# Four gate chunks computed inside the attention stage, and a weight product spread over its output chunks

## The reference

```python
for i in range(DEPTH):                       # DEPTH = 2
    shift, scale, gate = adaln_params(c, ada_w[i], ada_b[i])   # silu(c) @ w + b
    h = rms_norm(x, norm_g[i]) * (1.0 + scale) + shift
    # i = 0: q, k, v, g = split(h @ w_in); q, k normed and rotated;
    #        o = softmax over the last 128 keys, with a sink per head; branch = (o * silu(g)) @ w_out
    # i = 1: v, g = split(h @ w_in); pooled = trailing means of v over 2, 4, 8, 16 tokens, less v;
    #        mixed = einsum(pooled, w_group) * scale;  branch = (mixed * silu(g)) @ w_out
    x = x + gate * branch
```

## Time and profile before

| what | value |
|---|---|
| median of three runs | 1508.71 us (1503.67 to 1509.82) |
| the profiled execution's own time | 1503.65 us |
| its span, first to last instruction | 1501.9 us, mean granted clock 0.993 |
| TensorE busy | 1428.2 us, 95% of the span |
| gate stage's last matmul to slot 20 | 557.1 to 653.8 us of the span |

### The profile page before, as it was taken

The page is one execution under the profiler, slowest core; times in us unless marked ns, Lnnn a source line. Parts: engine busy times, 40 slices in busy tenths (PEclk is TensorE's granted clock), DMA queues, the critical chain, the costliest instruction groups (busy, mean ns, idle before and its releaser), DMA issues.

```text
span 1501.9 us, 20206 instructions
## 1 busy us (share of the span) xinstructions
PE 1428.2 (95%) x7240; PEld 1207.5 (80%) x7240; DVE 881.7 (59%) x1524; ACT 529.3 (35%) x1270; POOL 406.4 (27%) x551
## 2 busy tenths in 40 slices
PE   2899999999999998899999999899999999999999
PEld 1678888788778887888988988788888888888887
DVE  7777666765443449876776774525555443555522
ACT  2443443333311128765555562322213122221200
POOL 2333333321222216555655563310000100000000
PEclk9999999999999999999999999999999999999999
DMA  8655555434998788657767757731121552112142
GB/s 317 217 186 193 192 188 198 180 134 167 341 339 328 276 325 315 239 205 287 287 229 289 276 191 264 240 98 43 42 77 53 182 183 73 43 42 77 51 153 84
DMA packets 96787, 285.62 MB, mean 190 GB/s; under 512 B 10768, under 2 KB 40496, under 8 KB 87088
## 3 DMA queue, kind: packets, MB, share of 16 engines
q1 hardware_dynamic: 87760, 250.74, 46.2%
q0 software_dynamic: 8928, 33.59, 6.4%
HBM read 196.22 MB, written 88.08 MB: 189 GB/s over the span
## 4 chain that ended last, share of the span: by engine, by line
PE 71%; DMA 9%; DVE 8%; issue 5%; POOL 3%; ACT 3%; SPq 1%; POOLq 0%; DVEq 0%; ACTq 0%
PE po_f_ps L1841 23%; PE po_y_ps L1857 12%; PE at_y_ps L1413 9%; PE ga_g_ps L929 8%; PE qk_proj L663 7%; PE at_o_ps L1397 5%; PE at_s_ps L1369 3%; DMA values_split<-qk_late 3%; DMA ga_ada<-in_ada_w 2%; DMA po_xn<-x_mid_t 2%; POOL at_pt L1143 2%; PE at_tr L1379 1%; DMA ga_raw<-in_attn_w_gate 1%; POOL qk_rq L306 1%; DVE qk_late L476 1%
## 5 line engine op out<-in xcount | busy, mean ns | idle before, releaser
L1841 PE MATMUL po_f_ps<-po_ht,po_w 128*128 128x512 f32 x1536 | 348.9, 389 | 0.0
L1841 PEld LDWEIGHTS po_f_ps<-po_ht,po_w 128*128 128x128 f32 x1536 | 288.1, 188 | 60.1 <-DVE po_ht L1703 0.3
L663 PE MATMUL qk_proj<-qk_w_qkv,qk_ht 128*128 128x512 f32 x1152 | 280.4, 399 | 6.8 <-DVE qk_w_qkv L539 4.0
L663 PEld LDWEIGHTS qk_proj<-qk_w_qkv,qk_ht 128*128 128x128 f32 x1152 | 214.9, 190 | 53.9 <-issue 6.2
L1413 PE MATMUL at_y_ps<-at_zt,at_w 128*128 128x512 f32 x768 | 198.7, 400 | 6.2 <-DVE at_x L1302 6.2
L1857 PE MATMUL po_y_ps<-po_zt,po_w 128*128 128x512 f32 x768 | 174.7, 389 | 0.0
L1857 PEld LDWEIGHTS po_y_ps<-po_zt,po_w 128*128 128x128 f32 x768 | 144.1, 188 | 29.9
L1413 PEld LDWEIGHTS at_y_ps<-at_zt,at_w 128*128 128x128 f32 x768 | 138.5, 190 | 31.7 <-issue 7.4
L1143 POOL TENSOR_SCALAR_AFFINE_SELECT at_pt<-at_ph 128x512 fp32r<-128x512 f32 x128 | 96.7, 777 | 142.3 <-ACT at_ph L1196 137.0
L1690 DVE TENSOR_TENSOR po_w<-po_raw,po_w 128x1024 fp32r<-128x1024 f32 x48 | 58.8, 1225 | 128.7 <-ACT po_w L1624 128.7
L306 POOL TENSOR_TENSOR qk_rq<-qk_mq,qk_half 128x8 f32<-128x8 f32 (+1 forms) x48 | 70.2, 1463 | 177.2 <-DVE qk_mq L485 177.1
(11 more groups left out here) (168 smaller groups left out, 1968.0 us busy)
## 6 DMA issues: line engine op xcount, KB each, us to landing
at_w<-out_weight_split SPq DMA_DIRECT2D x32, 1024.0 KB, 6.0
queries_t<-qk_late SPq DMA_DIRECT2D x16, 1024.0 KB, 4.0
ga_ada<-in_ada_w POOLq DMA_DIRECT2D x64, 256.0 KB, 5.3
at_qt<-queries_t SPq DMA_DIRECT2D x16, 1024.0 KB, 8.2
ht_split<-qk_ht SPq DMA_DIRECT2D x6, 2048.0 KB, 9.6
values_split<-qk_late SPq DMA_DIRECT2D x16, 768.0 KB, 4.6
at_vs<-values_split SPq DMA_DIRECT2D x16, 768.0 KB, 5.0
qk_late<-in_ada_w SPq DMA_DIRECT2D x16, 512.0 KB, 5.3
```

The lines of the kernel that those rows point to most:

```text
L663: last = nc.tensor.matmul(proj[:, b * BANK:(b + 1) * BANK], ht[:, s % 2, m, k, t * P:(t + 1) * P], w_qkv[:, w, k, b * BANK:(b + 1) * BANK] ...
L1841: last = nc.tensor.matmul(f_ps[:, bank(j, h), :], w[:, i % 2, a, k, :], ht[:, h, m, k, :], start=(n == 0), stop=(n == 3 * KC - 1))
```

## The change

`gate_stage` computes only the first 28 chunks (`DENSE`). The last four, columns 4 to 7 of the last token block, are computed in the attention stage's slots 0 to 7: a chunk takes two slots, 12 matmuls in each, 6 ahead of the transposes and 6 behind them (`fill_product`). All four use one PSUM bank (`FILL_BANK`) and one SBUF buffer (`acc`), with a tanh, a silu and a store of their own in slots 2, 4, 6 and 8. Six of the 64 modulation pieces, the last `sum_mods` and `set_mods` move into slots 0 to 8 with them. The pieces of the output weight come two chunks earlier in the gate stage, the last at chunk 27, which is now the last one. The waits of the first eight gate chunks on the stage before are other ones, since the banks are numbered anew.

The fold is now 32 half-steps of 6 matmuls with a 128x256 result. Ten single ones (`LONE`) stand in slots 10 to 19; the other 22 stand in pairs in the second slot of output chunks 0 to 10 (slots 21, 23 to 41), in the bank of `y_ps` that the running chunk doesn't use.

```diff
-                ga["gpsimd"](pool)
+                ga["gpsimd"](pool, at["first_consts"])
...
+    FILL = KC // 2
+    DENSE = SLOTS - FILL
+    LAST = ORDER[NSB - 1]
...
+    FIRST_BANKS, RING_BANKS, FILL_BANK = (6, 0, 1, 2), (6, 3, 4, 5), 6
+
     def g_bank(q):
-        return g_ps[:, (q + 2) % 4, :]
+        if q >= DENSE:
+            return g_ps[:, FILL_BANK, :]
+        return g_ps[:, FIRST_BANKS[q] if q < 4 else RING_BANKS[q % 4], :]
 
     def out_piece(q):
-        return (q - KC) // 3 if q >= KC and (q - KC) % 3 == 0 and (q - KC) // 3 < KC else None
+        return (q - 6) // 3 if q >= 6 and q % 3 == 0 and q < DENSE else None
...
+        for q in range(KC // 2, DENSE):
             if q % KC == 0:
-                store(q // KC - 1)
+                store(q // KC - 1, KC)
...
-        store(NSB - 1)
-
-    def gpsimd(pool):
-        def load_ada(n):
-            layer, col = JOBS[n // KC]
-            wait(pool, ada_added, n - 3)
-            pool.dma_start(ada[:, n % 4, :], ada_w[layer][n % KC * P:(n % KC + 1) * P, col:col + BANK]).then_inc(ada_loaded[n % 4], 16)
-
+        store(NSB - 1, FILL)
...
+        for q in range(4, DENSE):
             for n in range(ada_by(q - 1) + 4, min(ada_by(q) + 4, ADA)):
-                load_ada(n)
+                load_ada(pool, n)
             if out_piece(q - 1) is not None:
                 store_out(out_piece(q - 1))
+            if q == DENSE - 2:
+                next_consts(pool)
+        store_out(KC - 1)
...
+    def fill_product(pe, n, ks):
+        q, f = DENSE + n, FILL + n
+        if ks[0] == 0:
+            pe.wait_ge(silu_done, q if n > 0 else DENSE - 3)
+        for k in ks:
+            for w, m in PRODUCTS:
+                last = nc.tensor.matmul(g_bank(q), split_of(f, w)[:, k * P:(k + 1) * P], ht[(NSB - 2) % 2][:, m, k, :],
+                                        start=(k == 0 and (w, m) == PRODUCTS[0]), stop=(k == KC - 1 and (w, m) == PRODUCTS[-1]))
+        if ks[-1] == KC - 1:
+            last.then_inc(g_done, 1)
+
+    def fill_tanh(act, n, out):
+        act.wait_ge(g_done, DENSE + n + 1)
+        wait(act, fill_stored, 16 * n)
+        nc.scalar.activation(out, g_bank(DENSE + n), ACT.Tanh, scale=0.5).then_inc(tanh_done, 1)
+
+    def fill_silu(dve, n, out):
+        dve.wait_ge(tanh_done, DENSE + n + 1)
+        nc.vector.scalar_tensor_tensor(out, out, 1.0, g_bank(DENSE + n), ALU.add, ALU.mult).then_inc(silu_done, 1)
+
+    def fill_store(sp, n, out):
+        f = FILL + n
+        sp.wait_ge(silu_done, DENSE + n + 1)
+        sp.dma_start(sg_d[PER * LAST:PER * (LAST + 1)][:, :, f * P:(f + 1) * P].rearrange("n p t -> p n t"),
+                     out.rearrange("p (n t) -> p n t", n=PER)).then_inc(fill_stored, 16)
...
+            elif q < 8:
+                pe.wait_ge(*((qk["norm_done"], 3 * NB), (qk["act_ev"], 2 * NB), (qk["dve_ev"], 2 * NB), (qk["k_lo"], NB))[q - 4])
...
-    ROWS = 2 * P
-    PAIRS = D // ROWS
-    FOLDS = GROUPS * PAIRS
+    PER_GROUP = D // P
+    FOLDS = GROUPS * PER_GROUP
+    FILL, FILL_SLOTS = ga["fill"], HALVES * ga["fill"]
+    FOLD_FROM = FILL_SLOTS + 2
...
+    LONE = first_slot(0) - FOLD_FROM
+    PAIRS = (FOLDS - LONE) // 2
+
+    def fold_slot(v):
+        return FOLD_FROM + v if v < LONE else first_slot((v - LONE) // 2) + HALVES - 1
+
+    def folds_in(i):
+        return [v for v in range(FOLDS) if fold_slot(v) == i]
+
+    def fold_bank(v):
+        return v % 2 if v < LONE else ((v - LONE) // 2 + 1) % 2
+
+    def fold_out_of(v):
+        side = 0 if v < LONE else v % 2 * GC * P
+        return y_ps[:, fold_bank(v), side:side + GC * P]
+
+    def folds_until(v):
+        return v + 1 if v < LONE else v + 2 - v % 2
...
+            if i == 0:
+                sp.wait_ge(ga["wo_stored"], 16 * KC)
+                load_sg(sp, 0)
+                load_sg(sp, 1)
+            if i in range(HALVES, FILL_SLOTS + 1, HALVES):
+                ga["fill_store"](sp, i // HALVES - 1, acc[:, :])
+            for v in folds_in(i - 1):
+                store_fold(sp, v)
+            for v in folds_in(i + 2):
+                load_fold(sp, v)
+            if i in range(FILL_SLOTS + 1, FILL_SLOTS + 4):
+                load_w(sp, i - FILL_SLOTS - 1)
...
+            if i in range(HALVES, FILL_SLOTS + 1, HALVES):
+                ga["fill_tanh"](act, i // HALVES - 1, acc[:, :])
             if i < UNITS:
                 previous(i)
-            if 0 <= i - 3 < FOLDS:
-                fold_evict(i - 3)
             if 1 <= i <= UNITS:
...
+            for v in folds_in(i):
+                fold_evict(v)
+            for v in folds_in(i + 1):
+                fold_high(v)
...
+            if i in range(HALVES, FILL_SLOTS + 1, HALVES):
+                ga["fill_silu"](dve, i // HALVES - 1, acc[:, :])
+            if i == FILL_SLOTS:
+                ga["set_mods"](dve)
...
-            if i < FOLDS:
-                fold_low(i)
+            for n in ga["ada_left"][i:i + 1]:
+                ga["add_ada"](dve, n)
+            for v in folds_in(i + 1):
+                fold_low(v)
...
-                if c < 2:
-                    pe.wait_ge(fold_out, FOLDS)
+                if c <= PAIRS:
+                    pe.wait_ge(fold_out, LONE + 2 * c if c > 0 else LONE - 1)
...
+        def fold(v):
+            pe.wait_ge(fold_lo, wv_split(v))
+            if v == 0:
+                pe.wait_ge(ga["silu_done"], ga["slots"])
+            elif v == 1:
+                pe.wait_ge(ga["mod_set"], 2)
+            else:
+                pe.wait_ge(fold_out, v - 1 if v < LONE else v - v % 2)
+            if v > LONE + 1:
+                pe.wait_ge(x1_done, (v - LONE) // 2)
             i = 0
             for c in range(GC):
                 for a, m in PRODUCTS:
-                    last = nc.tensor.matmul(fold_ps[:, u % 2, h].rearrange("p c n -> p (c n)"), wv[:, u % 3, a, c, h * P:(h + 1) * P],
-                                            wg[:, f % 2, m, c, :], start=(i == 0), stop=(i == 3 * GC - 1))
+                    last = nc.tensor.matmul(fold_out_of(v), wv[:, v % 2, a, c, :], wg[:, m, c, :],
+                                            start=(i == 0), stop=(i == 3 * GC - 1))
                     i += 1
-            if h == 1:
-                last.then_inc(fold_done, 1)
+            last.then_inc(fold_done, 1)
+
+        def fill(i, half):
+            if i < FILL_SLOTS:
+                k = i % HALVES * 2 * quarter + half * quarter
+                ga["fill_product"](pe, i // HALVES, list(range(k, k + quarter)))
...
-            if 0 <= i - 2 < FOLDS:
-                fold(i - 2, 0)
+            fill(i, 0)
             for c, k in part:
                 output(c, list(range(k, k + quarter)))
             if 2 <= i <= UNITS + 1:
                 p_round(i - 2)
-            if 0 <= i - 2 < FOLDS:
-                fold(i - 2, 1)
+            for v in folds_in(i):
+                fold(v)
+            fill(i, 1)
+            if i == FILL_SLOTS - 1:
+                ga["sum_mods"](pe, ga["jobs"] - 1)
```

More of the change, by code:

```diff
@@ L804, in sync, with store @@
     def sync(sp, next_load):
[L805 to L808, removed]
+        def store(j, chunks):
+            sp.wait_ge(silu_done, KC * j + chunks)
+            sp.dma_start(sg_d[PER * ORDER[j]:PER * (ORDER[j] + 1)][:, :, 0:chunks * P].rearrange("n p f -> p n f"),
+                         sg[:, :, 0:chunks, :].rearrange("p n k t -> p n (k t)")).then_inc(sg_stored, 16)
         for i in range(RAW + 2, KC + RAW):
             load(sp, i)
-        for q in range(KC, SLOTS):
+        for q in range(KC // 2, DENSE):
             if q % KC == 0:
-                store(q // KC - 1)
+                store(q // KC - 1, KC)
                 if q // KC + 1 < NSB:
@@ L861, in lo, with load_ada @@
         nc.vector.tensor_tensor(split_of(i, LO), raw[:, (RING0 + i) % RAW], split_of(i, HI).bitcast(F32), ALU.subtract).then_inc(w_lo, 1)
[L863 to L872 removed]
+    def load_ada(pool, n):
+        layer, col = JOBS[n // KC]
+        wait(pool, ada_added, n - 3)
+        pool.dma_start(ada[:, n % 4, :], ada_w[layer][n % KC * P:(n % KC + 1) * P, col:col + BANK]).then_inc(ada_loaded[n % 4], 16)
@@ new lines, in tanh, with silu @@
+    def tanh(act, q):
+        act.wait_ge(g_done, q + 1)
+        if q % KC == 0:
+            wait(act, sg_stored, 16 * (q // KC))
+        nc.scalar.activation(sg[:, :, q % KC, :], g_bank(q).rearrange("p (n t) -> p n t", n=PER), ACT.Tanh,
+                             scale=0.5).then_inc(tanh_done, 1)
+    def silu(dve, q):
+        dve.wait_ge(tanh_done, q + 1)
+        nc.vector.scalar_tensor_tensor(sg[:, :, q % KC, :], sg[:, :, q % KC, :], 1.0, g_bank(q).rearrange("p (n t) -> p n t", n=PER),
+                                       ALU.add, ALU.mult).then_inc(silu_done, 1)
@@ new lines, in sum_mods @@
+    def sum_mods(pe, j):
+        if j == 0:
+            pe.wait_ge(consts_set, 1)
+            pe.wait_ge(qk["hx_done"], KC * NB // 2)
+        pe.wait_ge(ada_added, KC * (j + 1))
```

(20 more changed lines are left out.)

234 lines of the change are left out of this document (110 added, 124 removed).

## The result

| kernel | median us | lowest to highest | runs |
|---|---|---|---|
| before | 1505.24 | 1502.04 to 1509.82 | 8 |
| after | 1516.79 | 1512.09 to 1526.98 | 8 |

The ratio is 1.0089, 95% interval 1.0071 to 1.0106: 13.4 us slower by it, 11.6 by the medians. The profiled execution took 1516.93 us, its span is 1515.2 us.

What follows compares the result with a forecast made beforehand. TensorE, busy for 95% of the span, was taken as the bound. Gate chunks -21.9, slots 0 to 19 +0.0 and pairs +15.8 gave -6.1 us, so 1508.7 would become 1502.6 us; range 1496 to 1512.

Steps and rivals of the forecast that it cites:

- the last sentence on the output slots: Output slots: SP issues four more small DMAs per pair, two chunks ahead of any need of the output weight.
- Four gate chunks: Gate stage, ahead of the first scores: removing four chunks gives back 21.93 us, on the path in full.
- Slots 0 to 7: Attention slots with the added gate matmuls: 40.0 us in all, with 38.2 as the lower bound.
- three handovers: Slots 2, 4, 6: next chunk waits for tanh and silu to free the shared bank; 2.9 us for three, bare 1.1.
- Slots 8 and 9: Attention slots with a silu, tiny operations and two splits on VectorE: 10.0 us for both.
- Slots 10 to 19: Attention slots with half the former fold each: 4.6 us each plus 0.7 in slot 17, 46.7 us together.
- Pairs: Output slots: 22 half-steps in pairs add 1.44 us in each of eleven slots, 15.8 us, all paid.
- Rival B: Slots 10 to 19: GpSimd's masks block VectorE's subtractions, 5.3 us each instead of 4.6, total 1509.6 us; chance 0.18.
- Rival C: Slot 4: tanh waits for the first added chunk's late store, up to 7.4 us, total 1510.0 us; chance 0.10.
- Rival D: Output slots: each pair delays the next chunk another 0.5 us by late eviction or split, total 1508.1 us; chance 0.08.
- Rival A: Slots 0 to 19: waits vanish as filling keeps TensorE going, 93.0 us, change -9.8 us, total 1498.9 us; chance 0.22.
- My 0.04 for slower: Whole kernel: chance 0.04 of measuring slower by more than 7.5 us, above 1516.3 us.

Runs made afterwards that it cites:

- late x load: Changed kernel with SP's load of x moved behind the block's values and gates and into the next slot: 1504.01 us, ratio 1.0006 to before.
- spread: Changed kernel with the first three loads of output weight and x issued in slots 9, 13 and 17 instead of 9, 10 and 11: 1512.47 us.
- late x and spread: Changed kernel with the edits of late x load and spread together: 1497.35 us, ratio 0.9947 to before.
- both edits: Changed kernel with late x load, and with fold results stored by ScalarE behind its evictions instead of by SP: 1506.01 us, ratio 1.0016 to before.

## Why the prediction was wrong

The failing step is the last sentence on the output slots: "SP issues four more small DMAs for each pair, two chunks ahead of any need of the output weight." I asked who needs the output weight, and never who needs the four DMAs themselves, nor what stands ahead of them on SP. Two waits did: ScalarE's eviction needs the earlier half-step's store landed, and ahead of that store SP waits for the residual's store. That cost 13.7 us (late x load: 12.8 back). The same omission stands in the part on slots 10 to 19, "its buffer has been stored a slot before": issued a slot before, but behind 4 MB, at a cost of 5.1 us against my 4.6 (spread: slot 14 from 9.68 to 4.45; with the late load, 4.22). Both are one mistake, a transfer counted as cheap by its size alone. A row had shown it: an eviction held up by 2.85 us before the change waited for just such a store, and I booked it as a stall that goes away.

Point by point:

- Four gate chunks, -21.9: right, in full.
- Slots 0 to 7, 40.0: measured 42.2. The term for three handovers was too small: slots 2, 4 and 6 took 6.70, 5.78 and 5.98 us for bare 4.06, 4.82 and 4.82, that is 4.8 us, not 2.9.
- Slots 8 and 9, 10.0: measured 8.4. Slot 8 took only 2.84 us, no more than its matmuls (0.96 + 0.36 + 1.53): TensorE waited for nothing there. That the long slot 7 let the softmax work run ahead is my reading of it.
- Slots 10 to 19, 46.7: 50.9 with the stall, 45.3 in the kernel without it, so halving the fold was priced 1.4 us too high.
- Pairs, 1.44 us each in eleven slots: right to the hundredth or two, 7.02 to 7.05 us for 5.60 (slot 37: 7.93 or 7.94 for 6.50) in every slot that holds one and has no stall, in all seven kernels with pairs.
- Rival B falls. The stretched subtraction came in about half of the slots, and did no harm. VectorE's timeline in slot 15 of the kernel with late x and spread, and two starts of scores on TensorE, of slots 15 and 16:

```profile
610.99 0.84 DVE L1395 TENSOR_TENSOR at_wv<-at_wv_raw,at_wv 128x256 fp32r<-128x256 f32 x1
...
610.12 1.12 PE L1458 MATMUL at_s_ps<-at_kt,at_qt 128*128 128x256 f32 x8
...
614.52 1.13 PE L1458 MATMUL at_s_ps<-at_kt,at_qt 128*128 128x256 f32 x8
```

- Slots 15 to 17 of that kernel are 4.21 to 4.40 us long with a subtraction of 0.83 or 0.84 in each, below even the bare 4.45 that I had taken as a floor.
- Rival C, the late store ahead of slot 4, showed as a wait of 1.13 us of ScalarE, not 7.4, and cost nothing: TensorE's wait behind it was 0.61 us, and also 0.61 in the kernel with both edits, where ScalarE did not wait for that store. Rival D named the right symptom, a late eviction, spread evenly at 0.5 us. It was lumpy instead: nothing behind seven of the pairs, 1.04 to 7.30 us behind the other four.
- Rival A, the waits vanish, did not happen in slots 0 to 7.

Without the two queue stalls the sum is -21.9 - 0.8 + 15.8 = -6.9 us (95.90 us from slot 0 to 20 against 96.73, with the last 0.81 of sums in both), and the kernel built that way measured -7.5 by medians. The forecast of -6.1 was thus near for the engines and blind to 13.7 + 5.1 = 18.8 us of the queue. That it was so near is partly luck: its three terms for slots 0 to 19 were off by +2.2, -1.6 and -1.4 us, and these nearly cancel. The range of 1496 to 1512 also hung on a median of three runs for the kernel before, 1508.7, where eight runs gave 1505.24; set 3.5 us lower it would have missed by more. My 0.04 for slower was too small for a reason to be seen ahead of time: I had listed what each engine is asked for, and no such list for SP.

## What to carry to other kernels

When work is moved to another loop, write down for each of its DMAs who waits for it, and what the issuing engine waits for ahead of it in program order; a 128 KB store behind a wait of 9 us is a store of 9 us and its landing. Put waits for landings (here a buffer's reuse) last in a slot's list of issues, and keep megabyte loads in slots of their own. If two repairs are to be summed, first ask whether they remove the same stall, and whether a stall that both leave has a second cause behind the first.

## What the runs showed of the hardware that was not expected

A wait grows when the clock falls in it, and not always. Slot 2 has the same wait for the handover in three kernels, 2.25, 2.25 and 2.31 us; it took 6.70 us in after, 8.26 with both edits and 8.32 with spread. Busy time in slot 2 of spread:

```profile
542.67:550.99 8.32, 6.01 (x25) 4.87 (x24) 6.79 (x12) 4.14 (x17) 2.41 (x5) 0.79 0.86 297
```

The granted clock was 0.79 there, and 1.00 in after's slot 2, with 4.45 us of TensorE's work instead of 6.01. So a stall that is 2.3 us by the waits can cost 1.6 us more. What decides between the two was not tried.

In the profiled run of the late x kernel slot 2 even took 10.59 us, by a cause that has nothing to do with its edit: ScalarE waited for a store of the output weight's pieces at the end of the gate stage, and VectorE and then TensorE for it. ScalarE's row:

```profile
538.53 1.06 ACT L864 ACTIVATE ga_wo<-ga_raw 128x1024 fp32r<-128x1024 f32 x1 [4.75 <-DMA out_weight_split<-ga_wo]
```

In the seven other kernels with the filling this wait was 2.0 to 2.4 us. My reading is that the filling has put TensorE's next need of VectorE so close to that store that its landing time now varies the kernel's; no run tests it, and what makes the landing vary was not tried.
